# A hybrid decoder layer on eight cores: three groups of transposes moved from TensorE to DMA

## The reference, cut to what matters

```python
h = rms_norm(x, pre_norm_g)
p = h @ w_in + b_in
q, k, v, g_attn, glu_val, glu_gate, g_conv = split(p)
q = partial_rope(q); k = partial_rope(k)            # 16 query heads, 2 key heads, 64 wide
attn = sliding_window_attention(q, k, v, sinks) * silu(g_attn)   # window 128, blocks of 128
conv = conformer_conv(glu_val, glu_gate, ...) * silu(g_conv)     # 31 taps per channel, layer norm, pointwise
x = x + rms_norm(concat([attn, conv]) @ w_out + b_out, post_norm_g)
```

## Time and profile before

| | |
|---|---|
| median of 3 runs | 1105.92 us (1105.06 to 1109.22) |
| the profiled execution's own time | 1108.99 us |
| its span (first to last instruction, slowest core, core 2) | 1107.5 us; the eight cores 1089.4 to 1107.5 us |
| busy on that core | PE 1034.8 us (93%), DVE 531.1 (48%), ACT 412.2 (37%), POOL 212.8 (19%) |
| granted TensorE clock, mean | 0.987 on core 2 |

### The profile page before, as it was taken

How to read it: one execution, slowest core, us unless ns; L and a number is a source line. 1 busy time by engine, 2 the same in 40 slices (tenths; PEclk the granted TensorE clock), 3 DMA queues, 4 the chain that set the end, 5 groups by cost and what they waited for, 6 DMA issues and landing times.

```text
span 1107.5 us, 17820 instructions; the slowest of 8 cores (1089.4 to 1107.5 us)
## 1 busy us (share of the span) xinstructions
PE 1034.8 (93%) x6848; PEld 543.7 (49%) x6906; DVE 531.1 (48%) x921; ACT 412.2 (37%) x1013; POOL 212.8 (19%) x215
## 2 busy tenths in 40 slices
PE   3799999899999999999999999989999999999996
PEld 1556444555555444445544644455655544444443
DVE  3566301466665355446636650045776636533434
ACT  2452112556555445034511212155565544402111
POOL 0260000134543320000000000012455341000000
PEclk9899999999999999999999999999999999999999
DMA  8874334655566589979499303344645657992445
GB/s 184 277 113 79 57 48 76 127 116 117 128 136 131 147 191 159 192 200 204 91 171 185 78 10 67 76 102 108 177 122 140 152 141 174 165 180 41 81 76 109
DMA packets 26533, 141.92 MB, mean 128 GB/s; under 512 B 5985, under 2 KB 6369, under 8 KB 15969
## 3 DMA queue, kind: packets, MB, share of 16 engines
q0 software_dynamic: 8784, 80.74, 43.1%
q1 hardware_dynamic: 17666, 60.04, 17.7%
HBM read 171.72 MB, written 32.51 MB: 184 GB/s over the span
## 4 chain that ended last, share of the span: by engine, by line
PE 73%; DMA 7%; SPq 6%; DVE 6%; ACT 3%; issue 3%; POOL 1%; ACTq 0%; DVEq 0%; POOLq 0%
PE psum L1144 19%; PE psum L775 10%; PE psum L1023 10%; SPq L152 6%; DMA arena<-arena 5%; PE psum L635 5%; PE psum L1113 5%; PE psum L869 4%; PE psum L818 4%; PE psum L828 4%; PE psum L631 3%; PE psum L593 2%; ACT arena L928 2%; PE psum L530 1%; PE psum L1182 1%
## 5 line engine op out<-in xcount | busy, mean ns | idle before, releaser
L1144 PE MATMUL psum<-arena 128*128 128x512 bf16 x939 | 207.2, 379 | 1.1
L1144 PEld LDWEIGHTS psum<-arena 128*128 128x128 bf16 x960 | 93.6, 98 | 111.3
L818 PE MATMUL psum<-arena 128*128 128x352 bf16 (+1 forms) x768 | 124.3, 316 | 0.0
L828 PE MATMUL psum<-arena 128*128 128x352 bf16 (+1 forms) x768 | 120.9, 311 | 3.4 <-ACT arena L831 3.3
L928 ACT ACTIVATE arena<-psum,arena 128x128 f32<-128x128 f32 x256 | 93.9, 367 | 61.4 <-DVE arena L918 43.6
L1023 PE MATMUL psum<-arena 128*128 128x512 bf16 x500 | 110.9, 379 | 4.3 <-ACT arena L1027 3.0
L775 PE MATMUL psum<-arena 128*128 128x512 bf16 x502 | 113.6, 387 | 0.5
L828 PEld LDWEIGHTS psum<-arena 128*128 128x128 bf16 x768 | 74.8, 98 | 42.9 <-issue 5.3
L818 PEld LDWEIGHTS psum<-arena 128*128 128x128 bf16 x768 | 72.5, 99 | 47.6 <-issue 12.7
L907 DVE COPY_PREDICATED psum<-arena,psum 128x1024 f32<-128x1024 uint16 x32 | 38.7, 1208 | 117.7 <-PE psum L901 117.7
L942 POOL TENSOR_TENSOR arena<-arena 128x1024 bf16<-128x1024 f32 x32 | 60.5, 1892 | 140.7 <-DVE arena L941 140.7
(11 more groups left out here) (129 smaller groups left out, 1282.9 us busy)
## 6 DMA issues: line engine op xcount, KB each, us to landing
arena<-w_in POOLq DMA_DIRECT2D x12, 2048.0 KB, 16.0
arena<-x_ext SPq DMA_DIRECT2D x18, 1024.0 KB, 10.6
arena<-w_in POOLq DMA_DIRECT2D x16, 1024.0 KB, 10.4
out<-arena POOLq DMA_DIRECT2D x15, 1024.0 KB, 9.2
arena<-w_out POOLq DMA_DIRECT2D x6, 2048.0 KB, 20.2
arena<-arena SPq DMA_DIRECT2D x64, 66.0 KB, 2.0
arena<-arena SPq DMA_DIRECT2D x64, 65.9 KB, 2.0
arena<-arena SPq DMA_DIRECT2D x64, 65.9 KB, 2.3
```

Of the source, the lines that this page charges most:

```text
L818: cx.op('pe', lambda e, k=k: e.matmul(out=bank[bv][:, 0:n], lhsT=wbuf.ap[:, k, o:o + 128], rhs=xv[:, k, st:st + n], start=(k == 0), stop=( ...
L828: cx.op('pe', lambda e, k=k: e.matmul(out=bank[bg][:, 0:n], lhsT=wbuf.ap[:, k, o + 128:o + 256], rhs=xv[:, k, st:st + n], start=(k == 0), ...
L1144: cx.op('pe', lambda e, k=k: e.matmul(out=bank[b], lhsT=MIX.ap[:, k, j * 128:(j + 1) * 128], rhs=wo[n][k][0].ap[:, wo[n][k][1], :], start= ...
```

## The change

Five things:

- The transposes of q (except g = 0 in the first half) and of k (second half only) are no longer done by PE and ACT; SP issues one DMA transpose for each, from the rope's buffer straight into MIX or kT.
- The transpose of a unit's softmax weights is a DMA transpose too (`att_d`): 128x1024 in bf16, SBUF to SBUF, on the SP queue. For even units it is issued in the tick of `att_n`; for odd units between the 12th and the 13th shuffle copy of the chunk.
- `att_t` keeps only the two mask multiplies, which now read SBUF. One of them works in place. It stands one tick later (2u + 5), and so does `att_o` (2u + 6); one more tick is run after `gconv(2)`.
- Bank 3, which held the PE transposes, joins banks 0 and 1 in the rotation of the GLU stage.
- The last tick of a chunk, and with it `att_n` of the odd unit, is now between the two parts of the shuffle in program order; the copy of x to the output comes after them.

```diff
-            def kv_b(j, kb):
+            def kv_b(j, kbn):
+                kb, n = kbn
+                if s == 1:
+                    cx.dma('sp', kT.ap[:, :, j * 128:(j + 1) * 128], kb.ap.rearrange("p g a d -> p (g a d)"), s_kt[n % 3],
+                           R=[kb], W=[kT_t[j]], transpose=True)
+                    return
...
-            def q_b(g, j, b_):
+            def q_b(g, j, bn):
+                b_, n = bn
+                if s == 1 or g == 1:
+                    cx.dma('sp', MIX.ap[:, 4 * g:4 * g + 4, (j - 1) * 128:j * 128], b_.ap, s_qt[n % 2],
+                           R=[b_], W=[mix_t[4 * g + t][j - 1] for t in range(4)], transpose=True)
+                    return
...
-            ptb = [mk(O_AT + 12288 + i * 2048, [8, 128], BF16) for i in range(2)]
+            ptb = mk(O_AT + 12288, [8, 128], BF16)
+            ptc = [mk(O_AT + o_, [8, 128], BF16) for o_ in (14336, 24576)]
...
-            rot["list"] = [0, 1]
+            rot["list"] = [0, 1, 3]
...
-            def conv_shuffle(c):
+            def conv_shuffle(c, part):
                 hg = hglu[c % 2]
-                for g in range(4):
-                    for i in range(4):
-                        cx.dma('sp', rs.ap[32 * i:32 * (i + 1), g, 0:HW - i], hg.ap[32 * g:32 * (g + 1), i:HW],
-                               s_rs, R=[hg], W=[rs], group=True)
+                for q in (range(12) if part == 0 else range(12, 16)):
+                    g, i = q // 4, q % 4
+                    cx.dma('sp', rs.ap[32 * i:32 * (i + 1), g, 0:HW - i], hg.ap[32 * g:32 * (g + 1), i:HW],
+                           s_rs, R=[hg], W=[rs], group=True)
...
+            def att_d(ui):
+                pu, pc = pn[ui % 2], ptc[ui % 2]
+                cx.dma('sp', pc.ap, pu.ap.rearrange("p h k -> p (h k)"), s_pt[ui % 2], R=[pu], W=[pc], transpose=True)
+
             def att_t(ui):
-                pu = pn[ui % 2]
-                for h in range(8):
-                    cx.op('pe', lambda e, h=h: e.transpose(
-                        out=bank_bf[TB][:, h * 128:(h + 1) * 128], in_=pu.ap[:, h, :], identity=ident_bf),
-                        R=[pu, idn], W=[BK[TB]])
-                for i, m in ((0, mprev_bf), (1, mcur_bf)):
-                    cx.op('dve', lambda e, i=i, m=m: e.tensor_tensor(
-                        out=ptb[i].ap, in0=bank_bf[TB].rearrange("p (h q) -> p h q", q=128),
-                        in1=m.unsqueeze(1).broadcast_to([128, 8, 128]), op=ALU.mult),
-                        R=[BK[TB], cst_bf], W=[ptb[i]])
+                pc = ptc[ui % 2]
+                for o_, m in ((ptb, mprev_bf), (pc, mcur_bf)):
+                    cx.op('dve', lambda e, o_=o_, m=m: e.tensor_tensor(
+                        out=o_.ap, in0=pc.ap, in1=m.unsqueeze(1).broadcast_to([128, 8, 128]), op=ALU.mult),
+                        R=[pc, cst_bf], W=[o_])
...
-                for lag_, f in ((5, att_o), (4, att_t), (2, att_n), (0, att_s)):
+                for lag_, f in ((6, att_o), (5, att_t), (2, att_n), (0, att_s)):
                     if (n - lag_) >= 0 and (n - lag_) % 2 == 0 and (n - lag_) // 2 < 16:
                         f((n - lag_) // 2)
+                        if f == att_n and n % 4 == 2:
+                            att_d((n - lag_) // 2)
...
-                conv_shuffle(c)
+                conv_shuffle(c, 0)
+                tick()
+                att_d(2 * c + 1)
+                conv_shuffle(c, 1)
                 if c < (NJ if s + 1 < NSUP else NJ - 1):
                     r0 = row0 + c * 128
                     cx.dma('sp', out_d[r0:r0 + 128, :], x_ext[r0 + HALO:r0 + HALO + 128, :], s_cp, W=[out_t[s * NJ + c]],
                            group=True)
-                tick()
...
             gconv(2)
+            tick()
```

More of the change, by code:

```diff
@@ L281, in build_program @@
         O_AT = O_CV + 17920
-        ARENA = O_AT + 24576
+        ARENA = O_AT + 26624
         arena = cx.sb("arena", [128, ARENA], U8)
@@ L372, in build_program @@
         s_x4 = cx.dsem("xr4")
+        s_qt = [cx.dsem("qt%d" % i) for i in range(2)]
+        s_kt = [cx.dsem("kt%d" % i) for i in range(3)]
+        s_pt = [cx.dsem("pt%d" % i) for i in range(2)]
         s_rs = cx.dsem("rs")
@@ L602, in kv_a @@
                     R=[kf], W=[V_t[j]])
-                return kb
-            def kv_b(j, kb):
+                return kb, n
+            def kv_b(j, kbn):
[4 more added lines that the diff above has]
+                    return
                 bt = nbank()
@@ L642, in q_a @@
                      8, s * 8 + j, r1, r2, [f], [b_], E, 'pool' if E == 'pool' else 'dve')
-                return b_
-            def q_b(g, j, b_):
+                return b_, n
+            def q_b(g, j, bn):
[4 more added lines that the diff above has]
+                    return
                 bt = nbank()
@@ L889, in conv_taps @@
                           R=[sb_, qss], W=[qss])
-            OB, TB = 2, 3
+            OB = 2
             SBK = [BK[i] for i in range(4, 8)]
@@ L944, in att_n @@
                     R=[eu, st["rden"]], W=[pu])
+            def att_d(ui):
+                pu, pc = pn[ui % 2], ptc[ui % 2]
+                cx.dma('sp', pc.ap, pu.ap.rearrange("p h k -> p (h k)"), s_pt[ui % 2], R=[pu], W=[pc], transpose=True)
             def att_t(ui):
-                pu = pn[ui % 2]
-                for h in range(8):
-                    cx.op('pe', lambda e, h=h: e.transpose(
-                        out=bank_bf[TB][:, h * 128:(h + 1) * 128], in_=pu.ap[:, h, :], identity=ident_bf),
-                        R=[pu, idn], W=[BK[TB]])
-                for i, m in ((0, mprev_bf), (1, mcur_bf)):
-                    cx.op('dve', lambda e, i=i, m=m: e.tensor_tensor(
-                        out=ptb[i].ap, in0=bank_bf[TB].rearrange("p (h q) -> p h q", q=128),
-                        in1=m.unsqueeze(1).broadcast_to([128, 8, 128]), op=ALU.mult),
-                        R=[BK[TB], cst_bf], W=[ptb[i]])
+                pc = ptc[ui % 2]
[3 more added lines that the diff above has]
+                        R=[pc, cst_bf], W=[o_])
             def att_o(ui):
                 g, j = units[ui]
+                pp = (ptb, ptc[ui % 2])
                 for kb in range(2):
@@ L966, in att_o @@
                                 out=bank[OB][32 * q4:32 * q4 + 32, :], lhsT=V.ap[:, kt, g, 32 * dq:32 * dq + 32],
-                                rhs=ptb[kb].ap[:, 4 * eh:4 * eh + 4, :].rearrange("p h q -> p (h q)"),
+                                rhs=pp[kb].ap[:, 4 * eh:4 * eh + 4, :].rearrange("p h q -> p (h q)"),
                                 start=(kb == 0), stop=(kb == 1), tile_position=(0, 32 * q4)),
-                                R=[V_t[kt], ptb[kb]], W=[BK[OB]])
+                                R=[V_t[kt], pp[kb]], W=[BK[OB]])
                 cx.op('dve', lambda e: e.tensor_tensor(
@@ L1039, in superblock @@
             rot["list"] = [0, 1, 2, 3]
-            assert tk["n"] >= 36
             if s + 1 < NSUP:
@@ L1052, in superblock @@
             gconv(2)
+            tick()
+            assert tk["n"] >= 37
             for t2 in range(2):
```

## The result

The changed kernel takes 1139.19 us (median of 4 runs, 1132.73 to 1205.75), the kernel before 1105.49 us on the same chip (4 runs). The ratio is 1.0284, 95% interval 1.0224 to 1.0345: about 31 us slower, outside the range that I gave.

What follows compares the result with a forecast made beforehand. PE was taken as the bound in most places, with a shuffle loop beside it in the GLU stage. Terms 6.8 + 4.4 + 0.8 + 6.0 - 7.2 gave 10.8 us less: 1095 us, range 1076 to 1124.

Steps and rivals of the forecast that it cites:

- The cover is the rope's double buffer (a transfer may take two periods, 7 us) and eight PSUM banks behind it.: q and k stages: 24 added q transfers of 128 KB, one each 3.5 us, stay hidden from PE.
- The bias of k: Start of k, second half: its load moves to about 613 us, lands near 624, hidden; far end 5 us lost.
- q and k on PE: q and k stages: removed PE transposes save 6.2 us, plus 0.6 us of rope waits, 6.8 us.
- X: GLU stage, SP's queue: time a softmax transpose holds SP, taken as 2 to 3 us, hidden up to 4.0 us.
- the slower rival: GLU stage: transposing transfers are expensive, deciding once X passes 5.5 us; 1119 us if 8 us; chance 0.25.
- T: GLU stage: what two added transfers cost the shuffle loop each period, 0.6 us, 7.2 us in total.
- masks and att_o one slot later: 0: Attention units: att_o sits beside att_s and its gate multiply still has a whole tick, so no cost.
- PE's own pace: GLU stage: PE's own work per period after the change, 20.1 us in the second half, 20.5 in the first.
- The third bank: GLU rotation: removes at most 5.4 us of PE waits on ACT, 0.8 us of it outside the periods.
- POOL held up by masks: 0: GLU stage: masks running beside POOL's odd-unit multiply could delay the weight load, up to 10.2 us; counted 0.
- The no-change rival: Whole kernel: the shuffle loop, POOL delay or k's bias takes the gain, 1101 to 1111 us; chance 0.14.

Runs made afterwards that it cites:

- d1: The changed kernel, but the last three stores of the first half write without adding: 1106.2 us, ratio 1.0032.
- a1: The changed kernel with q's chunk g = 0 of the second half transposed by PE and ACT again: 1103.9 us, ratio 1.0004.
- b1: The kernel before with only q's chunk g = 1 moved to DMA transposes, in both halves: 1094.1 us, ratio 0.9905.
- c1: a1 with the odd unit's softmax transpose issued behind all 16 shuffles instead of 12: 1095.9 us, ratio 0.9922.
- a2: The changed kernel with q's chunk g = 0 of the second half moved by plain copies, untransposed: 1108.1 us in the profiled execution.
- c3: a1 with each softmax weight transpose replaced by two plain copies, untransposed: 1101.8 us, ratio 0.9986.
- e2: The kernel before with q's g = 1 and second-half k by DMA, and the tap diagonals' multiply ahead of the third GLU group: 1092.8 us.
- e1: c1 with the DVE multiply for the tap diagonals issued ahead of the chunk's third GLU group: 1087.1 us, ratio 0.9853.
- c4: c1 with only banks 0 and 1 in the GLU rotation: 1096.5 us, ratio 0.9931.
- d2: The changed kernel, but the second half's first transpose waits until the first half's last three stores have landed: 1109.1 us, ratio 1.0033.
- c6: c1 with the GLU stage's weight loads issued only after the shuffles of the chunk before have landed: 1129.3 us, ratio 1.0194.

## Why the prediction was wrong, step by step

**The step that failed: "The cover is the rope's double buffer (a transfer may take two periods, 7 us) and eight PSUM banks behind it."** I had added the 24 q transfers to queues priced from rows of the GLU stage, and asked what each does there. Eight of them meet another company: three 1 MB stores that add, and two weight loads. There the first two took 32.5 and 50.0 us and not 7, and slowed the load of k's weights from 9.2 to 33.4 us; PE waited 22.7 us for those weights. Without these eight, 1103.9 instead of 1139.2 us. The row that should have made me stop was in my hands: the earlier trace rows, a plain load of 128 KB that took 11.1 us beside two of these stores. I priced k's bias with it and not the transposes that stand in the same window.

**The bias of k: "hidden, with 4 us to spare".** Not quite hidden. d1 is the case that I had described: on core 3 the bias is issued at 608.6, beside the 2 MB load, and lands 13.4 us later, at 622.0. DVE gets nothing of k done before, and PE waits 1.2 us at the end of its banks. In the changed kernel it was 1.6 us (core 5). The far end that I had given was 5 us.

**q and k on PE: 6.8 us.** Mis-sized, to the good side. Without the eight transposes of g = 0 my terms give 6.8 - 8 x 0.22 = 5.0 us; the stages of a1 give 4.0 + 1.7 + 5.7 = 11.4 us. The 0.22 us for a group is right. What I made too small was the estimate of 0.6 us for waits on the rope: when q changes chunk or ends, PE stood up to 2.1 us before a transpose that needed the rope, 5.9 us in four waits, and at one of these places lost another 1.7 us to the clock. b1 shows that most of the term pays in the whole kernel, 9.4 us.

**X, the transpose on SP: 2 to 3 us, hidden.** Right in size (2.93 us in the chunk shown, median 1.23 us, 4.98 at most; the slower rival asked for 5.5), wrong in "hidden": the four shuffles behind it landed later, as c1 shows. Of the two pages of the Trainium skill, a quiet queue bears out "Advanced Engine Details and Errata", X-Bar Transpose, by which it is as fast as plain: a q transpose with nothing beside it lands in 2.4 us, a plain copy of the same bytes in 2.3 (a2), and c3 is only 2 us from a1. The eight times 1309 ns of "VectorE: DVE Perf Modes", The three transpose paths, would be 10.5 us on the queue, an estimate from that page, and is not seen: the longest hold of SP is 4.98 us. Beside stores that add, "Advanced Engine Details and Errata" doesn't hold: the first two transposes take 22 to 56 us on the eight cores, the first two plain copies of a2 14 to 20.

**T = 0.6 us a period, 7.2 us.** Too small. The waits of conv_taps for shuffles rose from 9.4 to 30.8 us in both halves, where I had 15 to 20. The miss is in the second half: the period went to 23.15 us in the first, where I had 23.9, and to 23.63 in the second, where I had 21.3 (before on core 2, after on core 5). Place alone was 8 us of it (a1 to c1). The clock, which I had left out, adds to each long wait: the 4.1 us of busy time between cores 5 and 4 above.

**"masks and att_o one slot later: 0".** This is the second step that failed, and the one that ate what PE saved. I looked for who uses the result later, and not for what stands in front of the masks on DVE. In the changed kernel itself only 1.0 to 4.7 us of that wait are seen in the second half (cores 5 and 1), as the late shuffles cover it. Where they are out of the way it is 10.9 us (c1, core 0). With it mended, the transposes of the softmax weights pay, with the bank that they free: e2 to e1, 5.8 us.

**PE's own pace, 20.1 to 20.5 us.** e1 reaches 20.3 us in its best periods (starts of conv_taps on cores 0, 1 and 5), so the sum was right; only, nothing in the changed kernel could run at it. **The third bank, 0.8 us:** not seen in the kernel's time; on the slowest core its waits are taken by the shuffles (c4), while the GLU stages of the median core gain 4 to 6 us. **POOL held up by masks: 0.** L956 (the L942 of the earlier trace rows) has a median of 1892 ns against 1888, but a longest of 2345; its mean of 1921 makes 1 us over the kernel. Right for POOL; what it did to DVE stands below.

**The rivals.** The time fell on the slow side, but not by the slow rival's mechanism (X over 5.5 us). The no-change rival, "the loop takes all", gives a1's time, 1103.9, but by coincidence: there it is the loop, the masks and the gain of q and k together, and no 10 us on POOL.

## What to carry to other kernels

Price a moved transfer at every place where it is issued, by what is in flight there: one kind of transfer had three prices here: 2.4 us with nothing beside it, 7 to 16 us beside a 2 MB weight load, 22 to 56 us where it met stores that add. The dearest was paid by two of 64 on each core. When an operation moves to a later slot, list what now stands ahead of it on its own engine; a wait that another wait covers shows in the list as almost nothing until the other is gone. Count a long wait of PE more than once, as the clock that follows it can be lower. And when a change has several parts, separate them: q by DMA (-9 us by b1), softmax by DMA with its two orders mended (-6 us) and q's first chunk (+31 us, the ratios of a1 and the changed kernel) were all in it; the good ones together give 1087 us, 1.5% faster than before.

## What the hardware showed unexpectedly

- Transposing transfers and stores that add (1 MB each), in flight together: 32.5 and 50.0 us for two transposes of 128 KB, 33.4 us for a 1 MB load, and it went on for 34 us after the last store had landed, with the DMA engines at 23%. With stores that don't add (d1): 9.7 and 9.6 us for the first two transposes, 10.3 us for the load. With the transposes behind the stores (d2): 5.8 and 4.9 us, and 9.6 us.
- A multiply of 128x1024 bf16 on DVE takes the same with its operand in PSUM (683 ns in median, mean 685) and with both in SBUF: 692 ns, as shortest/median/longest say. Its mean there, 758 ns, comes from 4 of the 64. They took 1.6 to 2.3 us, and on every core it was four that ran while POOL added or multiplied (L902, L956), at the end of each half. In the earlier trace rows the same was seen on a small operation.

```profile
L967 DVE TENSOR_TENSOR arena<-arena x64: 681/692/2271, 211.8 to 934.7; 128x1024 bf16<-128x1024 bf16 x64
```

- The granted clock falls behind waits of PE, and it costs time after the wait is over. In c6 a stretch in which PE was busy for 2.06 of 4.60 us was followed by one in which PE worked throughout and the granted clock was 0.68 in the mean, part of it at 1.2 GHz and part at 2.4; in the 7.8 us behind it, with PE busy throughout, it was 1.00. Columns: window, its length, busy of PE, PEld, DVE, ACT and POOL, clock, DMA share, GB/s.

```profile
873.00:877.60 4.60, 2.06 (x36) 0.72 (x28) 2.93 (x4) 4.07 (x16) 1.49 (x2) 0.95 0.99 189
877.60:882.20 4.60, 4.56 (x28) 2.38 (x29) 3.82 (x5) 1.50 (x3) 4.60 (x4) 0.68 0.68 114
```
